# Routing by pairs of token tiles, half of the first gather between the pairs, and the norm's gain applied in the packed copies

## The reference

```python
h = h + (g_a * y_a + g_b * y_b) @ w_out[l]
hn = rmsnorm(h, norm_ffn_g[l])
h = h + hierarchical_moe(hn, ...)
...
glog = (xf @ w_rg + b_rg)
gsel = jnp.argmax(glog, axis=-1)
elog_all = (xf @ w_re + b_re).reshape(n, N_GROUPS, EXPERTS_PER_GROUP)
topv, topi = lax.top_k(elog, TOP_K)
tw = jax.nn.softmax(topv, axis=-1) * pg
for e in range(N_EXPERTS):
    h = jax.nn.silu(xf @ w_gate[e]) * (xf @ w_up[e])
    y = y + combine[:, e:e + 1] * (h @ w_down[e])
```

## Time and profile before

| what | value |
|---|---|
| time, median of 3 runs | 897.65 us (897.07 to 899.61) |
| the profiled execution | 897.03 us, of which the span of instructions 895.3 us |
| granted clock of PE, mean | 0.98 |
| PE busy | 848.3 us (95%) |
| DVE busy | 428.0 us (48%) |
| ACT busy | 231.9 us (26%) |
| moved by DMA | 250.03 MB, 279 GB/s in the mean |
| chain that ended last | PE 84%, DMA 10%, DVE 3%, ACT 1% |

### The profile page before, as it was taken

One profiled execution on the slowest core, in us unless ns is written; L12 is line 12 of the kernel. 1 busy time (PEld: TensorE's weight loads), 2 busy tenths in 40 slices (PEclk: granted clock), 3 DMA queues, 4 the chain that ended last, 5 costly groups with the idle time before them and its releaser, 6 DMA issues.

```text
span 895.3 us, 11458 instructions
## 1 busy us (share of the span) xinstructions
PE 848.3 (95%) x4635; PEld 550.1 (61%) x4635; DVE 428.0 (48%) x824; ACT 231.9 (26%) x423; POOL 7.6 (1%) x24
## 2 busy tenths in 40 slices
PE   8999999999999999999999969999995799999885
PEld 7888888877777888888844334544531443644532
DVE  5538325677675344436769144135133334335133
ACT  6322222464444222213304121100110100110124
POOL 0000000000000100000000000000000000000000
PEclk9999999999999999999999979999996999999998
DMA  8544312212222743696999999999999999999994
GB/s 292 153 94 112 102 48 94 94 48 76 67 94 57 216 136 94 236 388 245 367 383 346 415 429 428 425 427 428 427 429 428 426 428 428 427 426 428 428 410 191
DMA packets 72408, 250.03 MB, mean 279 GB/s; under 512 B 23032, under 2 KB 46624, under 8 KB 59168
## 3 DMA queue, kind: packets, MB, share of 16 engines
q1 hardware_dynamic: 71984, 248.18, 71.3%
q0 software_dynamic: 288, 1.05, 0.3%
q10 hardware_dynamic: 80, 0.02, 0.0%
HBM read 245.04 MB, written 4.20 MB: 278 GB/s over the span
## 4 chain that ended last, share of the span: by engine, by line
PE 84%; DMA 10%; DVE 3%; ACT 1%; issue 1%; SPq 0%; DVEq 0%; ACTq 0%
PE bank L1024 18%; PE bank L708 9%; PE bank L710 9%; PE bank L709 9%; PE bank L1083 8%; DMA R<-w_down 5%; DMA R<-w_gate 3%; PE bank L735 2%; PE bank L737 2%; PE bank L736 2%; PE bank L988 2%; PE by_side L988 2%; PE bank L1111 2%; PE bank L1070 2%; PE bank L1112 1%; DMA gate_fifth<-w_gate 1%
## 5 line engine op out<-in xcount | busy, mean ns | idle before, releaser
L1024 PE MATMUL bank<-R,packT 128*64 128x512 f32 (+1 forms) x972 | 187.0, 615 | 14.3 <-DMA R<-w_up 11.4
L1024 PEld LDWEIGHTS bank<-R,packT 128*64 128x64 f32 (+1 forms) x972 | 58.6, 130 | 124.5 <-issue 124.0
L1646 DVE TENSOR_TENSOR wlo<-raw,whi 128x2048 fp32r<-128x2048 f32 x33 | 75.5, 2288 | 84.8 <-ACT whi L1304 84.7
L708 PE MATMUL bank<-xnT_hi,whi 128*128 128x512 f32 x288 | 113.8, 395 | 0.0
L710 PE MATMUL bank<-xnT_hi,wlo 128*128 128x512 f32 x288 | 112.3, 390 | 0.0
L709 PE MATMUL bank<-xnT_lo,whi 128*128 128x512 f32 x288 | 112.2, 390 | 0.0
L1083 PE MATMUL bank<-R,actT 128*64 128x512 f32 (+1 forms) x384 | 75.2, 645 | 13.1 <-DMA R<-w_down 12.8
L1304 ACT ACTIVATE whi<-raw 128x2048 fp32r<-128x2048 f32 x33 | 63.0, 1910 | 66.9 <-PE by_side L710 33.8
L710 PEld LDWEIGHTS bank<-xnT_hi,wlo 128*128 128x128 f32 x288 | 54.1, 188 | 11.4
L708 PEld LDWEIGHTS bank<-xnT_hi,whi 128*128 128x128 f32 x288 | 54.1, 188 | 11.2 <-issue 0.6
L709 PEld LDWEIGHTS bank<-xnT_lo,whi 128*128 128x128 f32 x288 | 54.2, 188 | 10.7
(11 more groups left out here) (416 smaller groups left out, 1329.5 us busy)
## 6 DMA issues: line engine op xcount, KB each, us to landing
R<-w_up SPq DMA_DIRECT2D x27, 2048.0 KB, 21.3
R<-w_gate SPq DMA_DIRECT2D x25, 2048.0 KB, 21.2
R<-w_down SPq DMA_DIRECT2D x21, 2048.0 KB, 22.6
raw<-w_in SPq DMA_DIRECT2D x17, 1024.0 KB, 5.1
R<-w_down SPq DMA_DIRECT2D x12, 1024.0 KB, 13.8
R<-w_gate SPq DMA_DIRECT2D x14, 512.0 KB, 6.6
raw<-w_in SPq DMA_DIRECT2D x20, 256.0 KB, 4.6
R<-w_up SPq DMA_DIRECT2D x5, 1024.0 KB, 9.8
```

Of the source, the lines that this page charges most:

```text
L708: pe.matmul(dst, hi_w, hi_x, start=start, stop=False)
L1024: mm = pe.matmul(dst[s * w:(s + 1) * w, :], packT[:, side, c, s * w:(s + 1) * w], part_of(s, c) if part_of else slots[s // 2].tiles[s % 2] ...
L1646: dve.tensor_tensor(wlo[c % 2][:, :], raw[c % 2][:, :], whi[c % 2][:, :].bitcast(F32), ALU.subtract).then_inc(lo_split, 1)
```

## The change

Tiles 0 and 1 are routed ahead of tiles 2 and 3. PE turns tile 0 ahead of the last unit's tile 2, and turns tile 1 and makes the logits of both ahead of its tile 3. DVE chooses the experts, and makes the row numbers and masks, for one pair and then for the other: each instruction of that chain now runs twice, on two tiles. PE ranks each pair apart (`rank_tiles`), and gathers both halves of pair 0 (`gather_first(0, n)`) ahead of the ranks of pair 1; `gather_first(1, n)` follows the second pair's masks. `keep_warm` goes.

The gain leaves `hn_first`: `gain_h` and `ffn_g` go, `scale_h` on ACT reads `h_tok` and writes `hn_first` scaled by the root alone. The gain is applied in the copies to `packT`: four activations with a scale each on ACT, one multiply on DVE. The copies of transposed h are all on ACT. The stores of `hn_rows` are issued by ACT, two behind each pair's scaling, and no longer stand on SP's queue ahead of `gate_tail`. `gate_fifth` waits for the third mask.

```diff
             sp.dma_start(tenth[:, 4 * DE:8 * DE], flat(w_down, 1)[:, 4 * DE:8 * DE]).then_inc(slot_loaded[2], 16)
-            for t in range(TT):
-                sp.wait_ge(hn_ready, t + 1)
-                sp.dma_start(hn_rows[1 + t * P:1 + (t + 1) * P, :].rearrange("q (a n) -> q a n", a=2),
-                             hn_first[:, :, t, :, :].rearrange("q a c p -> q a (c p)")).then_inc(hn_stored, 16)
...
-            sp.wait_ge(masks_ready, 1)
+            sp.wait_ge(masks_ready, 3)
             sp.dma_start(gate_fifth[:, :], flat(w_gate, 0)[:, 4 * DE:5 * DE]).then_inc(fifth_loaded, 16)
...
-            def wide_unit(c, kh, xT_hi, xT_lo, done, before_last=None):
...
-                    if before_last and t == TT - 1:
-                        before_last()
+                    if t in ahead:
+                        ahead[t]()
...
-                    pe.wait_ge(hgT_a, t - 1)
-                    pe.wait_ge(hgT_b, t - 1)
+                    pe.wait_ge(hgT_copied, 2 * t - 2)
...
-                pe.wait_ge(hgT_a, t + 1)
-                if t < TT - 1:
-                    pe.wait_ge(hgT_b, t + 1)
-                else:
-                    pe.wait_ge(hgT_c, 1)
+                pe.wait_ge(hgT_copied, 2 * t + 2)
...
+                    mm = pe.matmul(logits_psum(t), hgT[t // 2][:, c, (t % 2) * P:(t % 2 + 1) * P],
...
-            def turn_first_tiles():
-                for t in range(2):
-                    turn_h(t)
+            def rank_tiles(pair):
+                pe.wait_ge(hgT_copied, 4)
+                pe.wait_ge(picked_ready, pair + 1)
+                for t in range(2 * pair, 2 * pair + 2):
+                    dst = ranks_psum[:, t * NE:(t + 1) * NE]
+                    pe.matmul(dst, all_ones[:, :], spaced_row[:, :], start=True, stop=False)
+                    for tp in range(t + 1):
+                        mm = pe.matmul(dst, earlier[:, :] if tp == t else all_ones[:, :],
...
+                mm.then_inc(ranks_done, 1)
+            def route_first_tiles():
+                turn_h(1)
+                pe.wait_ge(router_scaled, 1)
+                route(0)
+                route(1)
...
-                wide_unit(c, c % 2, mgT_hi, mgT_lo, dve_tile_done, turn_first_tiles if c == UNITS - 1 else None)
-            pe.wait_ge(router_scaled, 1)
-            route(0)
+                wide_unit(c, c % 2, mgT_hi, mgT_lo, dve_tile_done,
+                          {2: lambda: turn_h(0), 3: route_first_tiles} if c == UNITS - 1 else ())
             turn_h(2)
-            route(1)
+            pe.wait_ge(route_iotas_made, 13)
+            rank_tiles(0)
             turn_h(3)
             route(2)
...
-            def keep_warm(n):
-                for _ in range(n):
-                    pe.matmul(bank[4][:, :], ident[:, :], h_tok[:, 0, 0:512], start=True, stop=True)
-            keep_warm(3)
...
-            def gather_first(n):
-                for t in range(TT):
+            def gather_first(pair, n):
+                for t in range(2 * pair, 2 * pair + 2):
                     pe.wait_ge(masks_ready, t + 1)
                     for c in range(4):
                         mm = pe.matmul(bank[2 + n][:, c * P:(c + 1) * P], hn_first[:, n, t, c, :], onehot_first[:, t, :],
                                        start=(t == c == 0), stop=(t == TT - 1), skip_group_check=True)
-                mm.then_inc((left_turned, right_turned)[n], 1)
+                if pair:
+                    mm.then_inc((left_turned, right_turned)[n], 1)
...
-            for _ in range(3):
+            pe.wait_ge(h_ready, 2 * TT)
+            pe.wait_ge(hn_ready, 2)
+            for n in range(2):
+                gather_first(0, n)
+            fill(256, 4)
+            rank_tiles(1)
+            for t in range(TT):
+                mm = pe.matmul(bank[6][:, 0:NE], all_ones[:, :], picked[:, t, :], start=(t == 0), stop=(t == TT - 1))
+            mm.then_inc(ranks_done, 1)
+            for _ in range(2):
                 fill(256, 4)
             pe.wait_ge(hn_ready, TT)
-            gather_first(0)
+            gather_first(1, 0)
             number_rows(1, 1)
-            gather_first(1)
+            gather_first(1, 1)
...
-            def copy_hgT(t, half):
...
-                act.activation(hgT[t // 2][:, 4 * half:4 * half + 4, (t % 2) * P:(t % 2 + 1) * P],
-                               bank[4 + 2 * (t % 2) + half][:, :].rearrange("p (c q) -> p c q", c=4),
-                               ACT.Copy).then_inc(hgT_c if half else hgT_a, 1)
+                for half in range(2):
+                    act.activation(hgT[t // 2][:, 4 * half:4 * half + 4, (t % 2) * P:(t % 2 + 1) * P],
+                                   bank[HGT_BANKS[t][half]][:, :].rearrange("p (c q) -> p c q", c=4),
+                                   ACT.Copy).then_inc(hgT_copied, 1)
...
+            def scale_h(t):
+                act.wait_ge(rstd_ready, t // 2 + 1)
+                act.activation(hn_first[:, :, t, :, :], h_tok[:, t, :].rearrange("q (p a c) -> q a c p", a=2, c=KT // 2),
+                               ACT.Copy, scale=rstd[:, t:t + 1]).then_inc(hn_ready, 1)
+            def store_rows(t):
+                act.wait_ge(hn_ready, t + 1)
+                act.dma_start(hn_rows[1 + t * P:1 + (t + 1) * P, :].rearrange("q (a n) -> q a n", a=2),
+                              hn_first[:, :, t, :, :].rearrange("q a c p -> q a (c p)")).then_inc(hn_stored, 16)
...
-                act.wait_ge(rstd_ready, t // 2 + 1)
-                act.wait_ge(hg_ready, TT + t + 1)
-                act.activation(hn_first[:, :, t, :, :], hn_first[:, :, t, :, :], ACT.Copy,
-                               scale=rstd[:, t:t + 1]).then_inc(hn_ready, 1)
...
-            copy_hgT(0, 0)
-            copy_hgT(1, 0)
+            copy_hgT(0)
+            copy_hgT(1)
             square_h(1, 2)
             scale_h(0)
             scale_h(1)
+            store_rows(0)
+            store_rows(1)
+            copy_hgT(2)
             square_h(1, 3)
-            copy_hgT(2, 0)
-            copy_hgT(3, 0)
-            copy_hgT(3, 1)
+            copy_hgT(3)
             scale_h(2)
             scale_h(3)
+            store_rows(2)
+            store_rows(3)
...
+                    act.wait_ge(late_loaded, 16 * 5)
...
-                if r < 3:
-                    act.activation(packT[:, 0, 4 * n:4 * n + 4, :], bank[b][:, :].rearrange("p (c q) -> p c q", c=4),
-                                   ACT.Copy).then_inc((main.pack_a, main.pack_b)[n], 1)
-                    return
                 for c in range(4):
-                    last = act.activation(packT[:, 1, 4 * n + c, :], bank[b][:, c * P:(c + 1) * P], ACT.Copy,
+                    last = act.activation(packT[:, r // 3, 4 * n + c, :], bank[b][:, c * P:(c + 1) * P], ACT.Copy,
                                           scale=gain_pc[:, 4 * n + c:4 * n + c + 1])
...
-            def gain_h(n, t):
-                half = slice(n * 512, (n + 1) * 512)
-                dve.wait_ge(h_ready, TT * n + t + 1)
-                dve.tensor_tensor(hn_first[:, :, t, :, n * 64:(n + 1) * 64].rearrange("q a c p -> q p a c"),
-                                  h_tok[:, t, half].rearrange("q (p a c) -> q p a c", a=2, c=KT // 2),
-                                  ffn_g[:, half].rearrange("q (p a c) -> q p a c", a=2, c=KT // 2), ALU.mult).then_inc(hg_ready, 1)
...
-            dve.wait_ge(late_loaded, 16 * 6)
...
-            for t in range(TT):
-                gain_h(0, t)
...
-            add_h(1, 0)
-            gain_h(1, 0)
-            add_h(1, 1)
-            gain_h(1, 1)
-            norm_h(0)
-            add_h(1, 2)
-            copy_hgT(0)
-            copy_hgT(1)
-            gain_h(1, 2)
-            add_h(1, 3)
-            gain_h(1, 3)
-            copy_hgT(2)
-            norm_h(1)
...
+            def read_logits(t):
+                dve.wait_ge(logits_done, t + 1)
+                dve.scalar_tensor_tensor(out=logits[:, t, :], in0=logits_psum(t), scalar=rstd[:, t:t + 1], in1=b_router[:, :],
+                                         op0=ALU.mult, op1=ALU.add).then_inc(logits_ready, 1)
...
+            def choose(pair):
+                ts = slice(2 * pair, 2 * pair + 2)
+                dve.wait_ge(logits_ready, 2 * pair + 2)
+                places(place_g[:, ts, :], glog[:, ts, :], NG)
...
+                then(dve.tensor_scalar(chosen_8[:, ts, :], place_8[:, ts, :], 2.0, None, ALU.is_lt))
+                in_chosen_group(picked[:, ts, :], chosen_8, ts).then_inc(picked_ready, 1)
...
+            def spread_choices(pair):
+                ts = slice(2 * pair, 2 * pair + 2)
+                then(dve.tensor_scalar(first_8[:, ts, :], place_8[:, ts, :], 1.0, None, ALU.is_lt))
...
+            def first_masks(pair):
+                dve.wait_ge(choices_spread, 4 * pair + 2)
+                dve.wait_ge(ranks_done, pair + 1)
+                pick_rows(ranks, slice(2 * pair, 2 * pair + 2))
+                for t in range(2 * pair, 2 * pair + 2):
```

(26 more changed lines are left out.)

127 lines of the change are left out of this document (45 added, 82 removed).

## The result

The change made the kernel slower. Its median is 905.89 us (905.21 to 907.07, 4 runs) against 898.11 for the kernel before beside it (897.07 to 899.61, 4 runs): a ratio of 1.0087, interval 1.0068 to 1.0105. Forecast were 898.9 us and a range up to 901.8. The profiled execution took 905.92 us, with a span of 904.1, which is 8.8 us more than before.

A forecast was written before the change was run, and what follows sets the result against it. From 515 us on a saturated expert-weight stream bounds it, set by when c=4 is reached: +1.1 there and 0.2 for a copy, +1.3 on 897.03 gives 898.3; the median is 0.6 above, 898.9 us; range 895.4 to 901.8.

The forecast's parts named there:

- Which point decides: First expert's gate projection reaching chunk c=4 sets the end; forecast to move from 451.5 to about 452.6 us.
- The stores: Row stores on ScalarE's queue get half to a third of the bandwidth, taking 4.9 to 7.4 us plus some 2.
- rival B: Stores starve beside SP's queue, land 11.8 us after issue at 451.3; c=4 at 456.0, time 902.4 us; chance 0.14.
- The clock: With `keep_warm` gone, gathered pair 0 fills that stretch and TensorE's granted clock should stay at 1.00.
- The sum: At c=4 of the first gate projection: from 451.5 to about 452.6 us, +1.1; with 0.2 for copies, +1.3 in all.
- Tile 3 and the loads: SP's 3 MB behind the last unit's tile 3 leave at 428.3 instead of 424.95; `gate_fifth` lands at 452.7.
- Rival C: The 3.4 us DMA gap at 425 us is never repaid, so the weight stream ends later: 901.0 us; chance 0.11.
- the load of `ffn_g`: Dropped load, taken to stand at 310 us where the DMA share is 3 tenths: worth nothing.
- The gather and DVE's chain: Last route ends 434.3, second pair's first mask at 439.9, gather ends at 443.9, 3.8 us earlier; row numbers read at 442.6.
- one of the signs: Prediction wrong if the second pair's masks are off 439.9 by over 1 us.
- the scale: `scale_h` on ScalarE reading `h_tok` with a stride of eight elements: 2.1 us each instead of 1.15.
- The wait ahead of the first projection: TensorE waits 3 to 6 us there for the left copy or a store.

The follow-up runs named there:

- pairs_right_sooner: Changed kernel reordered as in pairs_only, with the right copy also made ahead of the sort's last reduction: 896.35 us, ratio 0.9986 to the kernel before.
- fills_r6late: Changed kernel with two 256-column products between the routes of each pair and the `R[6]` load issued behind `gate_fifth`: 897.83 us.
- fills_warm: Changed kernel with two 256-column products between each pair's routes and six 512-column products between the gather and first projection: 903.36 us.
- r6_late: Changed kernel with the 2 MB load of `R[6]` issued behind `gate_fifth` instead of ahead of it: 898.39 us.
- routes_behind2: Changed kernel with routes 0 and 1 behind the last unit's tile 3, h's last addition before the first choice, pair 0's ranks between routes 2 and 3: 903.73 us.
- before_gain_in_copies: Kernel before with `gain_h` removed, the scale reading `h_tok` with a stride and the gain in the copies; stores still on SP: 897.63 us.
- route_fills: Changed kernel with two unused 256-column products between the two routes of each pair: 905.09 us.
- pairs_only: Changed kernel with the order of routes_behind2, two 256-column products ahead of route 3, and `R[6]` loaded behind `gate_fifth`: 897.73 us.
- stores_sp: Changed kernel with the four row stores issued by SP behind its 3 MB of loads and ahead of `gate_tail`: 902.81 us.

## Why the prediction was wrong

**Which point decides** was right. From c=4 = 452.6 on the kernels order by it: 452.84 gives 898.39, 455.80 gives 902.81, 456.82 to 456.92 give 903.4 to 903.7, 458.5 to 458.6 give 905.0 and 459.79 gives 905.89, 7.5 us for 6.95. Nearer to the kernel before the medians differ by less than the runs can tell, but for pairs_right_sooner.

**The stores** were the step that failed. "They land at 446.4 to 448.9" rested on a share of a half to a third of the bytes from the issue on. Beside `R[6]` they got 0.01 MB up to 442 us, a tenth of the bytes from 442 to 446, a quarter over 440 to 450, and landed at 452.1. With `R[6]` behind `gate_fifth` the last store takes 6.6 us (fills_r6late), near the 4.9 + 2 of the forecast; with it, 12.06 (changed kernel). The issue itself was as said, 439.5 forecast and 440.0 found. That is rival B's mechanism: it took 11.8 us from issue to landing and put the landing at 451.3 and c=4 at 456.0, where fills_warm, with the clock kept, has 452.0 and 456.82. It had a chance of 0.14. Its own paragraph said that the row with the larger packets would get more than half, and that 2 MB of `R` stand in SP's queue; the sum went by a half to a third of the bytes all the same.

**The clock** was missed altogether. "The granted clock should stay": it fell three times. `keep_warm` and the turns between the routes had been removed, and what took their place was judged by whether PE is busy. The third fall comes behind the wait for the stores, is gone when the wait is filled (fills_warm), and costs 1.8 to 2.9 us at c=4 (458.61 against 456.82; 6.34 us for the four chunks against 3.45); rival B had not counted it. The first two move the gather's end from 446.2 to 449.3 and cost nothing here, as the stores are later still. The Trainium skill (TensorE: Matmul & The Clock Gate, Part 1: The HAM clock gate) ties the granted clock to how busy PE has lately been and warns of idle gaps. The third fall agrees; in the first two the profile shows no gap, and with products of 256 columns between the routes the clock stayed in all four runs that have them.

**The sum** at c=4 closes: the start of the projection +5.82, the slow clock in it +2.89, less the 0.44 that PE lost ahead of c=4 before and does not lose now (451.52 less 447.63 and 3.45), make 8.27.

**Tile 3 and the loads.** Forecast 428.3, found 430.24, of which the slow clock makes 1.4: in r6_late, where it held behind routes 0 and 1, the loads leave at 428.83. `gate_fifth` was forecast at 451 to 453 and landed at 451.9, though it left only at 445.10, behind a third mask that was 5 us late. Rival C's mechanism, a gap that the stream carries to its end, isn't there: in r6_late the loads leave 3.9 us later than before and the time is the same (898.39 against 897.92). What late loads do cost is the landing of the stores, 2.5 us in routes_behind2. That the load of `ffn_g` stood at a share of 3 tenths was misread (it is issued at 299.5 us, and its slice shows 7); before_gain_in_copies drops it and shows no difference.

**The gather and DVE's chain.** The last route ended at 436.3 for 434.3, the gather of pair 0 took 6.5 us for 3.6, and the second pair's first mask was ready at 445.1 for 439.9. That is off by over 1 us, one of the signs that the prediction had named for being wrong. With the clock kept (route_fills) these are 436.0, 3.7 and 442.0, and the token numbers are read at 444.35 for 442.6. But route_fills pays 1.9 us on PE for the products that keep the clock. Taken off, as an estimate, they give 434.1, 440.1 and 442.5, close to the forecast. So the chain was worked out rightly for a clock that stays; what it left out is that the clock falls in this order, and what it costs to keep it. In pairs_only, with one pair of such products and another order on DVE, `picked` is ready only at 440.4: first pair's masks, `norm_h(1)` and second choice stand in a row on DVE. Either way the gather ends at 446.1 to 446.8 and not at 443.9, the right copy comes no sooner than before, and the change is worth nothing that these runs can tell (fills_r6late, pairs_only).

**Right**: the scale at 2.17 us for 2.1, the left copy at 1.14 for 1.13, the multiply in the right copy at 0.69, and that bringing the gather forward gains nothing while the stores decide. The wait ahead of the first projection, 4.14 us for 3 to 6, came out right by luck: the gather's end and the stores were each 3 to 6 us later than forecast.

## What to carry to other kernels

A transfer that is moved to another engine's queue leaves its place in the order. Here the stores then shared with what the old queue issued, about packet for packet, and the small packets lost against the large ones. So look at which large load leaves just ahead of such a transfer, and try that one behind it. And when the order of narrow products is changed, look at the granted clock as a resource: a busy PE was not enough to keep it here, and the wait that the stores left was paid a second time in the clock of what followed.

## What was not expected of the hardware

Beside a load of 2 MB with 13.9 KB packets, stores with 2.0 KB packets got 0.16 of 1.58 MB in 4 us. PE's granted clock fell to 0.50 while its rows show no idle time, in passes of 36 columns; with one pair of products of 256 columns (0.95 us) between two such groups it stayed at 1.00.

What decides the first two falls stays open. Two routes in a row are not enough: the kernel before has routes 2 and 3 in a row too, from 429.98 to 433.6, at 1.00,

```profile
429.98 1.87 PE L918 MATMUL bank<-w_router,hgT 128*128 128x36 f32 x16
```

and before_gain_in_copies, with the same order on PE, falls to 0.56 behind them. r6_late and stores_sp kept the clock behind routes 0 and 1, where the changed kernel, with the same instructions on PE up to there, lost it. Nor are they needed: in routes_behind2 other products and 0.50 us of idle time stand between routes 2 and 3, and the clock fell behind route 3.
